# Moving the dot products with gathered rows of u from the U stage of the expert layer into its V stage, with four row buffers

## What is computed

```python
def blk(xb):
    ...
    sc, pos = lax.top_k(cand, PEER_TOPK)
    idx = jnp.take_along_axis(cidx, pos, axis=-1)
    gw = jax.nn.softmax(sc.astype(jnp.float32), axis=-1)
    act = jax.nn.gelu(jnp.einsum('thkd,td->thk', jnp.take(u, idx, axis=0), xb).astype(jnp.float32))
    return jnp.einsum('thk,thkd->td', (gw * act).astype(xb.dtype), jnp.take(v, idx, axis=0))
```

## Time and profile before

| | us |
|---|---|
| median of 3 runs | 2488.92 (2488.32 to 2498.36) |
| the profiled execution | 2486.21 |
| its span, first to last instruction | 2484.4 |
| TensorE busy | 2305.5 (93%) |
| mean granted TensorE clock | 0.947 of full |

### The profile page before, as it was taken

One profiled execution on the slowest core, in us unless ns is written; L12 is line 12 of the kernel. 1 busy time (PEld: TensorE's weight loads), 2 busy tenths in 40 slices (PEclk: granted clock), 3 DMA queues, 4 the chain that ended last, 5 costly groups with the idle time before them and its releaser, 6 DMA issues. The chain is left out here.

```text
span 2484.4 us, 58392 instructions
## 1 busy us (share of the span) xinstructions
PE 2305.5 (93%) x20464; PEld 2091.6 (84%) x20484; DVE 1523.3 (61%) x3131; ACT 1234.5 (50%) x2355; POOL 1073.5 (43%) x1000
## 2 busy tenths in 40 slices
PE   5966999999999999999979679999999999999998
PEld 4943777999998889999979238689999987999997
DVE  3466634993553976776554756359645459676765
ACT  3530113557545965555544302145674469555554
POOL 0004102885675844444200141058757767444431
PEclk8966899999999999999989688999999999999999
DMA  7556123555885057777444560345568830777763
GB/s 267 166 172 215 57 87 125 181 178 199 283 295 187 0 186 245 253 247 238 158 154 156 189 216 3 111 153 178 183 230 281 294 102 21 258 246 253 249 214 104
DMA packets 123816, 455.49 MB, mean 183 GB/s; under 512 B 13744, under 2 KB 14256, under 8 KB 122544
## 3 DMA queue, kind: packets, MB, share of 16 engines
q1 hardware_dynamic: 105264, 386.80, 44.2%
q0 software_dynamic: 18432, 67.12, 10.4%
HBM read 449.37 MB, written 4.49 MB: 183 GB/s over the span
## 5 line engine op out<-in xcount | busy, mean ns | idle before, releaser
L402 POOL TENSOR_TENSOR parts<-ring,parts 128x512 fp32r<-128x512 f32 x358 | 488.4, 1367 | 399.9 <-ACT parts L395 383.7
L395 ACT ACTIVATE parts<-ring 128x512 fp32r<-128x512 f32 x616 | 385.9, 631 | 387.0 <-PE ps_u L449 219.1
L445 PE MATMUL ps_u<-h_parts,parts 128*128 128x256 f32 x4096 | 566.1, 280 | 5.8 <-ACT parts L395 5.1
L2536 PE MATMUL ps_y<-act_parts,parts 128*128 128x256 f32 x4096 | 562.0, 280 | 0.0
L445 PEld LDWEIGHTS ps_u<-h_parts,parts 128*128 128x128 f32 x4096 | 516.1, 188 | 10.1 <-ACT parts L395 8.6
L2536 PEld LDWEIGHTS ps_y<-act_parts,parts 128*128 128x128 f32 x4096 | 515.1, 188 | 0.7 <-ACT parts L2484 0.3
L2582 POOL TENSOR_TENSOR act_parts<-big,act_parts 128x256 fp32r<-128x256 f32 x256 | 216.3, 845 | 422.6 <-ACT act_parts L2565 422.6
L402 DVE TENSOR_TENSOR parts<-ring,parts 128x512 fp32r<-128x512 f32 x258 | 184.8, 718 | 339.2 <-ACT parts L395 196.3
L449 PE MATMUL ps_u<-h_parts,parts 128*128 128x256 f32 x2048 | 328.4, 282 | 7.5 <-POOL parts L402 5.0
L2540 PE MATMUL ps_y<-act_parts,parts 128*128 128x256 f32 x2048 | 321.6, 279 | 0.0
L449 PEld LDWEIGHTS ps_u<-h_parts,parts 128*128 128x128 f32 x2048 | 276.2, 189 | 16.7 <-POOL parts L402 14.4
(11 more groups left out here) (388 smaller groups left out, 2859.2 us busy)
## 6 DMA issues: line engine op xcount, KB each, us to landing
ring<-in_stream SPq DMA_DIRECT2D x570, 512.0 KB, 3.6
more_ring<-in_stream SPq DMA_DIRECT2D x126, 512.0 KB, 3.7
big<-in_stream SPq DMA_DIRECT2D x16, 512.0 KB, 12.2
out_state_out<-big SPq DMA_DIRECT2D x2, 1440.0 KB, 7.0
big<-in_state SPq DMA_DIRECT2D x2, 1280.0 KB, 11.2
big<-in_mixc SPq DMA_DIRECT2D x2, 1024.0 KB, 8.5
big<-in_spots SPq DMA_DIRECT2D x2, 1024.0 KB, 5.3
x_res<-in_x SPq DMA_DIRECT2D x1, 1152.0 KB, 5.4
```

Of the source, the lines that this page charges most:

```text
L395: eng.activation(m.parts[:, q % PARTS, 0, :], half_tile(m, t, half), ACT.Copy).then_inc(s["hi_ready"], 1)
L402: eng.tensor_tensor(m.parts[:, q % PARTS, 1, :], half_tile(m, t, half), m.parts[:, q % PARTS, 0, :].bitcast(F32), ALU.subtract).then_inc(m ...
L445: pe.matmul(out, hi[:, k, :], hr[:, side, kk, 0:tokens], start=(kk + side == 0), stop=False)
L2536: pe.matmul(ps[:, half * KD // 2 + k, :], hi[:, k, :], act_parts[:, j % AHEAD, side, :], start=False, stop=False)
```

## The change

The dots leave the U stage and go into the V stage, in turns 2 to 9; the adds follow in turns 11 to 18. Four row buffers take the place of two: the two of `m.rows`, and two of 1024 floats in activation columns 0 to 7, which the V stage has used up after tile 7. A turn of six tiles has four row operations, after tiles 1, 2, 4 and 5. GpSimd asks for a row right behind its subtraction of the tile whose row operation last uses the buffer, six tiles ahead of its use; it still waits for `row_used` of that buffer. The Gelu (ScalarE, before tile 60), the clearing of `m.tokens` (VectorE, before tile 60) and the product with the gates (VectorE, before tile 66) stand between the two series. Line 2336's operation and line 2624's are as before in size. In the U stage VectorE and GpSimd keep their halves of the splitting; the sample sum of TensorE moves from tile 114 to tile 120, and its use on VectorE from tile 120 to tile 126.

```diff
+ROWS = 4
...
-        self.dot_rows = Area(self.big, (NKEYS - 2 * D // NP) * NP).take(2, D)
...
 def experts_block(nc, m, l, hr, stream, spots_in):
...
-            each_tile(act, TURNED + RING, DOTS_END + RING, tile)
-            act.wait_ge(s["dots_ready"], 1)
-            act.activation(m.dot, m.dot, ACT.Gelu_apprx_tanh).then_inc(s["dots_out"], 1)
-            each_tile(act, DOTS_END + RING, NKEYS - 2, tile)
+            each_tile(act, TURNED + RING, NKEYS - 2, tile)
...
-            for turn in range(DOTS // RING - 1, DOTS_END // RING):
-                n = turn - DOTS // RING
-                for j in range(RING):
-                    first_half(turn, j)
-                    if j == 0 and n >= 0:
-                        fetch(n, 1)
-                    if j == 2 and n + 1 < HALF:
-                        fetch(n + 1, 0)
-            each_tile(pool, DOTS_END, NKEYS, first_half)
+            each_tile(pool, TOPK_TILES, NKEYS, first_half)
...
-            v.wait_ge(s["tokens_out"], 2)
-            each_tile(v, DOTS, DOTS_END, dot)
...
+            each_tile(v, SOFT + 2 * RING, NKEYS, second_half)
...
-def combine_block(nc, m, l, stream):
+def combine_block(nc, m, l, stream, u_rows):
...
+    OPS = SLOTS // ROWS
+    DOT = 2
+    DOT_END = DOT + OPS
+    ADD = DOT_END + 1
+    ADD_END = ADD + OPS
+    assert ADD_END < TURNS
...
+        def row(i):
+
+            return m.rows[:, i, :] if i < 2 else m.big[:, (i - 2) * D:(i - 1) * D]
+
+        def row_of(j):
+
+            return j // RING * 2 + j % RING - 1
...
-            each_tile(act, 0, NKEYS, tile, VRING)
+            each_tile(act, 0, VRING * DOT_END, tile, VRING)
+            act.wait_ge(s["dots_ready"], 1)
+            act.activation(m.dot, m.dot, ACT.Gelu_apprx_tanh).then_inc(s["act_ready"], 1)
+            each_tile(act, VRING * DOT_END, NKEYS, tile, VRING)
...
+            def fetch(table, index, n, i):
+
+                used = n if table is u_rows else OPS + n
+                if used:
+                    pool.wait_ge(s[f"row_used{i}"], used)
+                at = ROWS * n + i
+                pool.indirect_dma_start(row(i), None, table, bass.IndirectOffsetOnAxis(ap=index[:, at:at + 1], axis=0)).then_inc(
+                    m.fetched[i], 16)
 
             for turn in range(TURNS):
-                n = turn - ADD
                 for j in range(VRING):
                     tile(turn, j)
-                    if j == 0 and 0 <= n < HALF:
-                        fetch(n, 1)
-                    if j == 3 and 0 <= n + 1 < HALF:
-                        fetch(n + 1, 0)
+                    for table, index, at in ((u_rows, m.u_row, DOT), (v_rows, m.v_row, ADD)):
+                        if j % RING and 0 <= turn + 1 - at < OPS:
+                            fetch(table, index, turn + 1 - at, row_of(j))
...
+            def tile_dot(g, j):
+                tile(g, j)
+                if j % RING:
+                    i, n = row_of(j), g - DOT
+                    v.wait_ge(m.fetched[i], l * (2 * OPS * 16) + n * 16 + 16)
+                    v.scalar_tensor_tensor(row(i), row(i), 1.0, m.tokens, ALU.mult, ALU.mult,
+                                           accum_out=m.dot[:, ds(n * ROWS + i, 1)]).then_inc(s[f"row_used{i}"], 1)
+
             def tile_add(g, j):
                 tile(g, j)
...
+                if j % RING:
+                    i, n = row_of(j), g - ADD
+                    v.wait_ge(m.fetched[i], l * (2 * OPS * 16) + n * 16 + (OPS + 1) * 16)
+                    v.wait_ge(s[f"row_used{(i - 1) % ROWS}"], n + (OPS + 1 if i else OPS))
+                    v.scalar_tensor_tensor(m.tokens, row(i), m.dot[:, ds(n * ROWS + i, 1)], m.tokens,
+                                           ALU.mult, ALU.add).then_inc(s[f"row_used{i}"], 1)
+
+            each_tile(v, 0, VRING * DOT, tile, VRING)
+            each_tile(v, VRING * DOT, VRING * DOT_END, tile_dot, VRING)
...
+            v.sem_inc(s["dots_ready"], 1)
+            v.memset(m.tokens, 0.0).then_inc(s["weighted"], 1)
+            each_tile(v, VRING * DOT_END, VRING * ADD, tile, VRING)
+            v.wait_ge(s["act_ready"], 1)
+            v.tensor_tensor(m.dot, m.dot, m.weight, ALU.mult).then_inc(s["weighted"], 1)
+            v.wait_ge(s["weighted"], 2)
+            each_tile(v, VRING * ADD, VRING * ADD_END, tile_add, VRING)
```

More of the change, by code:

```diff
@@ L239, in __init__ @@
         self.loaded = [ctx.enter_context(nc.semaphore(f"tile_loaded{i}")) for i in range(RING)]
-        self.fetched = [ctx.enter_context(nc.semaphore(f"row_fetched{i}")) for i in range(2)]
+        self.fetched = [ctx.enter_context(nc.semaphore(f"row_fetched{i}")) for i in range(ROWS)]
         self.done = [ctx.enter_context(nc.semaphore(f"tile_done{i}")) for i in range(RING)]
@@ L2054, in _, with experts_block @@
                 mm.then_inc(m.done[t % RING], 1)
[L2057 removed]
+def experts_block(nc, m, l, hr, stream, spots_in):
     assert TOPK_TILES % RING == 0
     names = ("step score_ps score_out found act_out hi_ready lo_ready parts_used tokens_ps tokens_out "
[L2061 to L2062 removed]
+             "picked exp_ready gates_ready turned picks_ready spots_loaded")
     SCORES1, SCORES2, TOKENS = 2 * RING, 9 * RING, 10 * RING
     SOFT, TURNED = TOPK_TILES + 3 * RING, TOPK_TILES + 6 * RING
[L2065 to L2066 removed]
     GROUPS = ((HEADS, 0, m.sel[:, :, 0, :]), (HEADS, 1, m.sel[:, :, 1, :]), (HEADS // FOLD, 0, m.sel[:, :, 2, 0:SLOTS]))
@@ L2542, in tile @@
                     mm.then_inc(s["parts_used"], 1)
-            each_tile(pe, 0, VRING * (TURNS - 2), tile, VRING)
+            each_tile(pe, 0, VRING * (TURNS - 1), tile, VRING)
             pe.wait_ge(s["samples_ready"], 1)
@@ L2549, in _ @@
             mm.then_inc(s["samples_summed"], 1)
-            each_tile(pe, VRING * (TURNS - 2), NKEYS, tile, VRING)
+            each_tile(pe, VRING * (TURNS - 1), NKEYS, tile, VRING)
             for n in range(4):
@@ L2616, in tile_add @@
                 tile(g, j)
-                if j % RING == RING - 1:
-                    q, n = j // RING, g - ADD
-                    v.wait_ge(m.fetched[q], l * (2 * HALF * 16) + HALF * 16 + n * 16 + 16)
-                    if q:
-                        v.wait_ge(s["row_used0"], n + 1)
-                    else:
-                        v.wait_ge(s["row_used1"], n + 1)
-                    v.scalar_tensor_tensor(m.tokens, m.rows[:, q, :], m.dot[:, ds(n * 2 + q, 1)], m.tokens,
-                                           ALU.mult, ALU.add).then_inc(s[f"row_used{q}"], 1)
@@ new lines, in _ @@
+            each_tile(v, 0, VRING * DOT, tile, VRING)
+            each_tile(v, VRING * DOT, VRING * DOT_END, tile_dot, VRING)
+            for i in range(ROWS):
+                v.wait_ge(s[f"row_used{i}"], OPS)
+            v.sem_inc(s["dots_ready"], 1)
[3 more added lines that the diff above has]
+            v.tensor_tensor(m.dot, m.dot, m.weight, ALU.mult).then_inc(s["weighted"], 1)
@@ L2630, in _ @@
+            v.wait_ge(s["weighted"], 2)
+            each_tile(v, VRING * ADD, VRING * ADD_END, tile_add, VRING)
+            v.wait_ge(s[f"row_used{ROWS - 1}"], 2 * OPS)
             v.sem_inc(s["samples_ready"], 1)
-            each_tile(v, VRING * (ADD + HALF), VRING * (TURNS - 1), tile, VRING)
+            each_tile(v, VRING * ADD_END, VRING * TURNS, tile, VRING)
             v.wait_ge(s["samples_summed"], 1)
@@ L2637, in _ @@
             v.tensor_tensor(m.x[:, :, NP:NT], m.x[:, :, NP:NT], tmp[:, :, :], ALU.add).then_inc(s["x_ready"], 1)
-            each_tile(v, VRING * (TURNS - 1), NKEYS, tile, VRING)
+            each_tile(v, VRING * TURNS, NKEYS, tile, VRING)
             for k in range(KD):
```

30 lines of the change are left out of this document (5 added, 25 removed).

## The result

| | before | after |
|---|---|---|
| median, runs side by side | 2494.03 us (6 runs) | 2571.64 us (2568.23 to 2578.59, 6 runs) |
| ratio | | 1.0317, 95% interval 1.0297 to 1.0337 |
| profiled execution, its span | 2486.21, 2484.4 | 2578.59, 2576.8 |

A forecast was written before the change was run, and what follows sets the result against it. TensorE, busy 93% of the span, was taken as the bound, through its gaps and pace. -25.0 (U stage) + 25.8 (dots) + 45.6 (adds) = +46.4 us on 2486.2, plus 2.7 to the median: 2535 us; range 2482 to 2560.

The forecast's parts named there:

- U stage, 25.0 us: U stage: without dots and fetches, tiles 69 to 127 lose their gaps, a gain of 12.5 us a layer.
- Gelu, memset and small product: Operations leaving the U stage, where they were beside other work; in the V stage taken as zero, Gelu bounded by 3 us.
- DMA and VectorE's added work, zero: V stage: four row operations a turn still fit VectorE, and 312 GB/s of DMA demand costs nothing.
- The second rival: V stage: no change, as the wait costs little or DMA binds instead; 2487 to 2489 us, chance 0.10.
- The third rival: Still slower: fetches and waits join and DVE falls behind as well; over 2560 us, chance 0.05.
- The wait as the deciding term, with its place: V stage: GpSimd's fetch waits for the same tile's row operation, delaying the next subtraction and TensorE; 25.8 plus 45.6 us.
- The first rival: V stage: the wait stays under TensorE's need, tiles keep 2.80 us, only the U gain is left; 2464 us, chance 0.15.
- VectorE's splitting of A+1's second half: V stage, dots: splitting from 956.17 to 956.86 holds GpSimd to 956.72, so the subtraction ends at 957.45.
- A+1: V stage: the tile after the one followed in the prediction; its subtraction stands behind the waiting fetch on GpSimd's queue.
- group of three tiles: V stage: two tiles with row operations and a third without; 28 groups with dots, 28 with adds, in both layers.
- 1.63 + 0: V stage, adds: 1.63 us lost at the first waited fetch of a group, the next in time; 45.6 us in all.
- The lock: A VectorE operation and GpSimd's subtraction don't run together; the later one came free 0.14 us before the other's end.

The follow-up runs named there:

- late_fetch: The changed kernel with each row's fetch issued one tile later on GpSimd, as the kernel before does: 2467.48 us, ratio 0.991.
- eight_rows: The changed kernel with eight row buffers instead of four, fetches issued at the same places: 2468.18 us, ratio 0.9912.
- memset_behind: The changed kernel with a one-column GpSimd memset directly behind each fetch's issue, ahead of the next subtraction: 2584.91 us, ratio 1.0383.
- scalar_wait: The kernel with eight row buffers plus a wait for ScalarE's first copy of the next tile before each fetch: 2567.13 us, ratio 1.0308.

## Why the prediction was wrong in size and right in direction

**U stage, 25.0 us: right.** 26.4 in the trace, as all of the excess goes. Tiles 69 to 127 of layer 2 took 165.2 us where 178.2 were shown before. Gelu, memset and small product cost nothing that shows: TensorE is busy 20.00 of 20 us at 1060.

**DMA and VectorE's added work, zero: right.** 302 to 314 GB/s with TensorE never idle in the windows of `late_fetch` and `eight_rows`. The second rival's reading by DMA falls with it, and its reading by a small wait (0.44 us a group) falls by the 1.94 below. The third rival named the right band, over 2560 us, with another mechanism: VectorE does the same work in `late_fetch` and `eight_rows`, busy 83 to 88 of 100 us, and keeps up.

**The wait as the deciding term, with its place: right.** 112 waits of 2.4 us, issues 0.28 us behind the dot's end, gaps behind the subtraction, in those turns and the tile behind each series. The first rival fell.

**The size: wrong, in one step.** It was "VectorE's splitting of A+1's second half (956.17 to 956.86, 2.80 after A's at 953.37) holds GpSimd to 956.72, so it ends at 957.45". That step let the splitting run beside the issue. It started where it was put, 0.7 us into the issue, but took 1.21 us instead of 0.69 and ended 0.68 after the issue, ahead of the subtraction: that ends about 0.5 us later. With it both fetches of a group lose 0.97.

| group of three tiles | forecast | measured |
|---|---|---|
| dots | 0.44 + 0.48 = 0.92 | 1.94 |
| adds | 1.63 + 0 | 1.94 |
| turn with dots, with adds | 18.6, 20.1 | 20.7, 20.7 |

The adds were nearer for the wrong reason. Their issue was taken at 1.44 us, from 1.23 for the v table and 0.21 for waiting; it takes 1.17 at the median. The 1.23 belongs to the stage and not to the table: in `late_fetch` both tables' fetches take 1.23 at the median. So the add of A+1 doesn't get ahead of the subtraction, and the 1.63 of one tile doesn't arise; the splitting's delay does, at both. The 56 groups cost 108.6 us instead of 71.4. With that in place the forecast's own sum is 2486.2 - 25.0 + 108.6 + 2.7 = 2572.5 us, against 2571.6 measured.

**The lock.** The forecast let VectorE and GpSimd exclude each other only where a VectorE operation meets GpSimd's subtraction. In the kernel after, VectorE's instruction with two operands was held while the profile shows on GpSimd only the issue, and in `memset_behind` the issue and a memset; of these only the issue reads SBUF, its column of row numbers. The Trainium skill, SBUF — State Buffer, section "Who interferes with whom", has this contention only with a GpSimd instruction that reads SBUF, and infers that a tensor_tensor isn't in the way of descriptor generation. The trace agrees where the subtraction behind the issue isn't ready (0.69), and not where it is (1.20 to 1.29). The earlier trace rows held no such pair, and the range had no term for it. Why a subtraction that hasn't started by the profile makes the difference stays open.

## What to carry to other kernels

A fetch that must wait for its buffer doesn't belong on an in-order queue ahead of work that the busiest engine needs: ask for it one tile later, or give each row a second buffer. Here that decision alone was worth some 100 us (ratios of 1.0317 and 0.991 to the same kernel) and turned a loss of 3.2% into a gain of 0.9%. When a chain is costed by placing old instructions beside new ones, each overlap of two engines needs a row of its own, in the same situation: here a splitting took 0.69 us beside an issue with nothing to do behind it, and 1.21 beside one with the subtraction ready.

## What was unexpected of the hardware

- A splitting of VectorE that starts 0.56 us or more into the issue of an indirect fetch on GpSimd took 1.20 to 1.29 us instead of 0.69 wherever GpSimd's next subtraction was ready (but for the two 0.07 us before the issue's end), also with a memset in between, and 0.69 wherever it wasn't. One that started at most 0.27 us in took 0.69 with the subtraction ready (`scalar_wait`). Why is open. That GpSimd prepares its next instructions during the issue is a guess.
- A late operand costs TensorE more than its lateness: the subtraction ended at 949.86, 0.79 us after 949.07, and 0.97 was lost, so 0.18 beyond. The 0.16 taken from the earlier trace rows held.
- In the profiled execution of `late_fetch` layer 1 ran its V stage with 836 matmuls in 100 us instead of 860, without idle time and at a granted clock of 1.00 (372.4 us against 363.1 in layer 2). The pace was the same, 169 matmuls in 20 us, where the DMA share was 0.64 and where it was 0.92, so the load of the DMA engines doesn't explain it. The cause was not tried.
